# The prompt's last state built from the carried state: PE turns it back, ACT decays it, VectorE adds the second chunk's part

## The chip, the cores and the metric

One core of one Trainium2 chip runs the whole program. The metric is device time in microseconds (us), as the median of several runs. Below, PE is TensorE, DVE is VectorE, ACT is ScalarE, POOL is GpSimd, and SP is the queue that loads the weights.

## What is computed

One layer of a hybrid decoder: a Mamba-2 mixer beside a gated short convolution, then a gated ConvFFN and a gated per-layer embedding. There are 256 prompt tokens (one sequence, from a zero state) and 8 sequences of 8 sample tokens each, which makes 320 columns in all. The change concerns only the state that the prompt leaves behind. The prompt is worked off in two chunks of 128 tokens:

```python
decay_end = jnp.exp(Acum[:, :, -1:] - Acum)
chunk_states = jnp.einsum('bclgn,bclgr,bclgrp->bcgrpn', Bm, decay_end * dt, x)
chunk_decay = jnp.exp(Acum[:, :, -1])
def step(h, inp):
    s, d = inp
    return d[..., None, None] * h + s, h
hT, h_prev = lax.scan(step, h0.reshape(b, G, R, P, N), ...)
```

With a zero start and two chunks the last state is `hT = chunk_decay[1] * S0 + S1`, with S0 and S1 the two chunk states. S0 is also the state carried into the second chunk. There are 64 heads in 8 groups of 8. Per group a state has 512 rows (8 heads of 64) and 128 columns.

## The kernel before

All activations stand channel-major, so a projection is a matmul with a 128x128 block of weights held in the array and 320 token columns moving through. Weights come as f32 pieces of 128x1024. ACT rounds each piece to fp32r (`whi`, L670), DVE subtracts to get the rest (`wlo`, L1003), and PE does three matmuls for each block (L1567 to L1569). A `unit` is two such pieces, 48 matmuls, and gives 128 output channels.

The program is a hand-written list of steps (`ssm_steps`), which each engine walks through in its own block (`@block.scalar`, `@block.vector`, `@block.tensor` and so on). Each engine runs its part of a step in the order written there, and semaphores join them. The Mamba part is 8 rounds, one for each group of heads. Group 0 stands by itself and the other seven are a loop. A round ends with

`unit z0, ssd1, unit z1, ssd3, pair 0, unit z2, pair 1, unit z3, pair 2, pair 3`

- **dtab** (once, at the start): PE sums the decay exponents, ACT takes their exp, DVE multiplies. Kind 9 of `heads_tab` holds the weight of a first-chunk token in the last state: its PE sums go to bank 6 (two matmuls, L1880 and L1881), its exp is L852, its product with dt L1206.
- **ssd1**: PE turns x into rows of tokens. DVE scales them into `xdt` (for the output), `xwe` (for the end of their own chunk) and, for chunk 0 alone, `xwf` (for the end of the prompt, by kind 9).
- **ssd3**: PE turns the sample states of pair 0 (eight transposes, `turn_states`, L1774), makes the carried state S0 in bank 2 with one matmul of 512 columns (L1914), then the last state in bank 3, for each of four blocks of two heads `xwf` times chunk 0's B plus `xwe` times chunk 1's B (L1917, L1918: eight matmuls of 128 columns). ACT copies the turned states (L794), S0 into `h1t` (L906), the last state into `hfin` (L909), and issues its store (L911).
- **pair j** (two heads each): PE makes the outputs inside a chunk (L1931, bank 6), waits for `h1_kept` and `t_kept`, adds what the carried states give (L1942, L1946), and `carry_in` makes the samples' state updates in banks 7 and 2 (L1783). It then turns the next pair's sample states (L1774) and the pair's `yo` (L1955). ACT copies `yo` (L918) and the turned states, squares the pair's result, issues the load of the states two pairs on (L683) and the store of the new ones (L928). POOL decays the sample states (L1499), and DVE adds the update (L1256).

`HN_BANKS` is (7, 2): `carry_in` uses bank 7 for its first half and bank 2 for its second. `ea` holds, for each row of heads and each prompt column of chunk 1, exp of the running sum, so its column 127 is `chunk_decay[1]`.

Of the kernel before, what the change touches and what calls it, by code (L numbers as in the profile page):

```python
# [7 lines left out]
ACT = mybir.ActivationFunctionType  # L8

P = 128  # L10
# [3 lines left out]
NS = NB * LB  # L14
# [74 lines left out]
def ssm_steps(first):  # L89
    def x(*js):  # L90
        return [("unit", "x", j) for j in js]
    if first:
        head = (x(1) + [("dtend", 0)] + x(2) + [("dturn", 0)] + x(3) + [("dtab", 0)] + x(4)
                + [("bc", 0), ("decay", 0)] + x(5) + [("clamp", 0)])
        tail = [("unit", "z", 0), ("exps", 0), ("ssd1", 0), ("unit", "z", 1), ("mask", 0)]
    else:
        head = (x(0, 1) + [("norm", 0)] + x(2, 3) + [("bc", 0)] + x(4) + OUT8[:5] + [("decay", 0), ("clamp", 0)]
                + OUT8[5:6] + [("exps", 0)] + OUT8[6:] + [("mask", 0)] + x(5))
        tail = [("unit", "z", 0), ("ssd1", 0), ("unit", "z", 1)]
    return head + tail + [("ssd3", 0), ("pair", 0), ("unit", "z", 2), ("pair", 1), ("unit", "z", 3),  # L100
                          ("pair", 2), ("pair", 3)]

# [50 lines left out]
def hybrid_decoder(nc, ins, outs, scratch):  # L154
# [7 lines left out]
    with ctx:  # L162
        def sem(name):
            return ctx.enter_context(nc.semaphore(name))
# [38 lines left out]
        def s1(name, shape, dt=F32):  # L203
            return ssm.enter_context(nc.sbuf_tensor(name, shape, dt))

        N_KC = 10
        heads_tab = s1("heads_tab", [P, GROUPS, N_KC, HPG])
        hvec = s1("hvec", [HEADS, 3])  # L210
        dcol = s1("dcol", [P, HEADS // 2])
# [28 lines left out]
        cv = s1("cv", [P, 2, WX])  # L240
        xdt = s1("xdt", [P, 3, 4 * P])
        xwe = s1("xwe", [P, 3, 4 * P])
        xwf = s1("xwf", [P, 4 * P])
        bt = s1("bt", [P, 3, P])
        bblk = s1("bblk", [NS, NB // 2, P])
        cbm = s1("cbm", [P, 3, P])
# [111 lines left out]
        row_sums, rows_kept, rows_saved = sem("row_sums"), sem("rows_kept"), sem("rows_saved")  # L358
        acum_loaded, ea_loaded = sem("acum_loaded"), sem("ea_loaded")
        h1_done, h1_kept, hfin_stored = sem("h1_done"), sem("h1_kept"), sem("hfin_stored")  # L360
        h0_loaded = [sem(f"h0_loaded{i}") for i in range(2)]
        hn_stored = [sem(f"hn_stored{i}") for i in range(2)]
        t_done, t_kept = sem("t_done"), sem("t_kept")
# [30 lines left out]
        def at(i, n=1, size=1):  # L394
            return slice(i * size, (i + n) * size) if isinstance(i, int) else bass.ds(i * size, n * size)
# [255 lines left out]
        def _(act):  # L651
# [137 lines left out]
            def keep_states(g, j):  # L789

                wait(act, yo_done, 4 * g + j)
                for half in range(2):
                    act.wait_ge(t_done, 8 * g + 2 * j + half + 1)
                    activate(h0t[:, 4 * half:4 * half + 4, :].rearrange("p b n -> p (b n)"),  # L794
                             ps[:, 4 + half, :], copy).then_inc(t_kept, 1)

            def silu_x(g, i):

                act.wait_ge(conv_done, 6 * g + i + 1)

                wait(act, yg_ready, 4 * (g - 1) + (4 if i < 2 else i - 1))
                dst = bc[:, i, :] if i < 2 else xs[:, i - 2, :]
                activate(dst[:, 0:SEQ], prompt_of(cv[:, i % 2], K_X), ACT.Silu)
                if i == 1:
                    activate(c_own[:, :, :, 0:LB], samples_of(cv[:, i % 2], K_X).rearrange("p (h b) l -> p h b l", h=2),
                             ACT.Silu)
                activate(dst[:, SEQ:NT].rearrange("p (b l) -> p b l", l=LB), samples_of(cv[:, i % 2], K_X),
                         ACT.Silu).then_inc(xs_ready, 1)

            def tasks(seg, it, step, pos, outs_end):  # L810
# [34 lines left out]
                elif kind == "dtab":  # L845
# [2 lines left out]
                    activate(heads_tab[:, :, 3:5, :].rearrange("p g c h -> p c g h"),  # L848
                             ps[:, 5, 0:2 * HEADS].rearrange("p (c g h) -> p c g h", c=2, g=GROUPS), ACT.Exp)
                    activate(heads_tab[0:NS, :, 5, :],  # L850
                             ps[0:NS, 5, 2 * HEADS:3 * HEADS].rearrange("p (g h) -> p g h", g=GROUPS), ACT.Exp)
                    activate(heads_tab[:, :, 9, :],  # L852
                             ps[:, 6, 0:HEADS].rearrange("p (g h) -> p g h", g=GROUPS), ACT.Exp).then_inc(dt_decay, 1)
                    act.wait_ge(row_sums, 1)
                    activate(wm[0:HEADS, 2, 0:NT], ps[0:HEADS, 7, 0:NT], copy).then_inc(rows_kept, 1)
                    activate(wm[0:HEADS, 3, 0:P + NS + NB], ps[0:HEADS, 7, P:NT + NB], ACT.Exp).then_inc(rows_kept, 1)
# [41 lines left out]
                elif kind == "exps":  # L898
                    for quad in range(5):
                        act.wait_ge(q_pos, 5 * g + quad + 1)  # L900
                        part = wm[:, quad, :] if quad < 4 else wm[0:NS, quad, :]
                        activate(part, part, ACT.Exp, scale=-1.0).then_inc(q_exp, 1)
                elif kind == "ssd3":
                    keep_states(g, 0)
                    act.wait_ge(h1_done, 2 * g + 1)
                    activate(h1t[:], ps[:, 2, :], copy).then_inc(h1_kept, 1)  # L906
                    act.wait_ge(h1_done, 2 * g + 2)
                    wait(act, hfin_stored, 16 * g)
                    activate(hfin[:].rearrange("p q n -> p (q n)"), ps[:, 3, :], copy).then_inc(h1_kept, 1)  # L909
                    act.wait_ge(h1_kept, 2 * g + 2)  # L910
                    act.dma_start(outs["ssm_prompt"][0, 0].rearrange("h p n -> (h p) n")  # L911
                                  .rearrange("(q m) n -> m q n", m=P)[:, at(4 * g, 4)],
                                  hfin[:]).then_inc(hfin_stored, 16)
                elif kind == "pair":

                    wait(act, yoff_done, 4 * g + j)
# [1 line left out]
                    activate(yo[:], ps[:, YOFF_BANKS[j], P:2 * P], copy).then_inc(yo_kept, 1)  # L918
                    if j < 3:
                        keep_states(g, j + 1)  # L920
                    act.wait_ge(yg_ready, 4 * g + j + 1)
                    activate(zs[:, j, :], chunk[:, j, :], ACT.Square).then_inc(ysq_ready, 1)

# [70 lines left out]
        def _(dve):  # L994
# [167 lines left out]
            def tasks(seg, it, step, pos, outs_end):  # L1162
# [36 lines left out]
                elif kind == "dtab":  # L1199
# [5 lines left out]
                    tt(heads_tab[0:NS, :, 5, :], heads_tab[0:NS, :, 5, :], heads_tab[0:NS, :, 2, :], MUL)  # L1205
                    tt(heads_tab[:, :, 9, :], heads_tab[:, :, 9, :], heads_tab[:, :, 0, :], MUL  # L1206
                       ).then_inc(heads_ready, 1)
                elif kind == "unit" and step[1] == "x":
                    dve.wait_ge(xpad_filled, 6 * g + j + 1)
# [6 lines left out]
                elif kind == "ssd1":  # L1216
                    dve.wait_ge(hcol_ready, g + 1)
                    for c in range(3):
                        rows = P if c < 2 else NS
                        dve.wait_ge(xt_done, 3 * g + c + 1)  # L1220
                        xchunk(xdt[0:rows, c, :], c, hcol[0:rows, c, :], rows)
                        if c == 0:
                            xchunk(xwf[:], c, hcol[:, 9, :], rows)
                        xchunk(xwe[0:rows, c, :], c, hcol[0:rows, 3 + c, :], rows).then_inc(xw_ready, 1)
                elif kind == "bc":
                    dve.wait_ge(cb_done, g + 1)
# [9 lines left out]
                elif kind == "mask":  # L1236
                    dve.wait_ge(cbm_ready, g + 1)
                    for quad in range(5):
                        dve.wait_ge(q_exp, 5 * g + quad + 1)
                        c = CHUNK_OF[quad]  # L1240
                        rows, n = (P, 4) if quad < 4 else (NS, 8)
                        w3 = wm[0:rows, quad, :].rearrange("p (h n) -> p h n", h=n)
                        width = 512 // n
                        tt(w3, w3, cbm[0:rows, c, 0:width].unsqueeze(1).broadcast_to([rows, n, width]), MUL
                           ).then_inc(w_ready, 1)
                elif kind == "pair":
                    y = chunk[:, j, :]
                    dve.wait_ge(yd_done, 4 * g + j + 1)
# [313 lines left out]
        def _(pe):  # L1562
# [213 lines left out]

            def carry_in(g, j):

                for half in range(2):
                    if j:  # L1780
                        pe.wait_ge(hn_added, 8 * g + 2 * (j - 1) + half + 1)
                    rows = slice(half * NS // 2, (half + 1) * NS // 2)
                    mm(ps[:, HN_BANKS[half], :], xwe[rows, 2, j * P:(j + 1) * P],  # L1783
                       bblk[rows].rearrange("p b n -> p (b n)"), start=True, stop=True).then_inc(hn_done, 1)

            def tasks(seg, it, step, pos):
# [83 lines left out]
                elif kind == "dtab":  # L1870
# [5 lines left out]
                    for bank, inner, inner_s in ((4, tri[:], tri_s[:, 0:NS]), (5, after[:], after_s[:])):  # L1876
                        for c in range(2):
                            mm(ps[:, bank, c * HEADS:(c + 1) * HEADS], inner, dta(c, P), start=True, stop=True)
                        mm(ps[0:NS, bank, 2 * HEADS:3 * HEADS], inner_s, dta(2, NS), start=True, stop=True)
# [30 lines left out]
                elif kind == "ssd3":  # L1910
                    pe.wait_ge(xw_ready, 3 * g + 3)
                    pe.wait_ge(bt_kept, g + 1)
                    turn_states(g, 0)
                    mm(ps[:, 2, :], bt[:, 0, :], xwe[:, 0, :], start=True, stop=True).then_inc(h1_done, 1)  # L1914
                    for q in range(4):
                        cols = slice(q * P, (q + 1) * P)
                        mm(ps[:, 3, cols], xwf[:, cols], bt[:, 0, :], start=True, stop=False)  # L1917
                        last = mm(ps[:, 3, cols], xwe[:, 1, cols], bt[:, 1, :], start=False, stop=True)  # L1918
                    last.then_inc(h1_done, 1)
                elif kind == "pair":  # L1920
                    pe.wait_ge(w_ready, 5 * g + 5)
                    pe.wait_ge(cbm_ready, g + 1)
# [87 lines left out]
```

## Time and profile before

| | us |
|---|---|
| median of three runs | 2902.71 (2902.35 to 2904.03) |
| the profiled execution | 2901.83 |
| its span | 2900.1 |
| PE busy in the span | 2864.2 (99%) |
| DVE busy | 1718.3 (59%) |
| ACT busy | 1183.2 (41%) |
| POOL busy | 282.8 (10%) |

Busy time of PE is nearly the whole span. A matmul's row is longer than the step from one matmul's start to the next, since they overlap in the array. So what a matmul costs is read from starts, and a wait from a start that comes late.

### The profile page before, as it was taken

To read this page: it belongs to the slowest core of one execution; us is meant where nothing else is said; L and a number is where in the kernel's file an instruction comes from. 1 tells how busy PE (TensorE), PEld (TensorE's weight loads), DVE (VectorE), ACT (ScalarE), POOL (GpSimd) and SP (SyncE) were. 2 spreads that over 40 slices of the span, in tenths; PEclk is the share of its full clock that TensorE was granted. 3 is DMA by queue.
4 is the path that set the end of the run, shared out by engine and by line. 5 is a ranking of instruction groups with operands and counts; after the bars stand their busy time and mean duration, and the time that the engine had idled before them with its cause. 6 is when DMAs were issued, how large, how long until landed. Compare 5 with 4: busy or idle time off the path is not lost.

```text
span 2900.1 us, 52971 instructions
## 1 busy us (share of the span) xinstructions
PE 2864.2 (99%) x19924; PEld 2793.6 (96%) x19924; DVE 1718.3 (59%) x2165; ACT 1183.2 (41%) x1745; POOL 282.8 (10%) x447
## 2 busy tenths in 40 slices
PE   7999999999999999999999999999999999999998
PEld 6899999999999999999999999999999999999998
DVE  7676766767667655455455555655555555555564
ACT  4554544545445433333333334433333333333543
POOL 2211212112121200000000001000000000000100
PEclk9999999999999999999999999999999999999999
DMA  7666565665656655555555554555455555545463
GB/s 203 162 180 183 150 195 148 181 182 150 195 149 181 183 161 153 153 145 151 153 142 150 151 153 140 146 153 152 145 152 152 145 145 154 149 145 155 135 177 109
DMA packets 753280, 457.33 MB, mean 158 GB/s; under 512 B 14633, under 2 KB 747233, under 8 KB 752625
## 3 DMA queue, kind: packets, MB, share of 16 engines
q1 hardware_dynamic: 679433, 414.21, 50.5%
q10 hardware_dynamic: 73096, 39.39, 4.9%
q0 software_dynamic: 672, 2.66, 0.2%
q8 instruction: 52, 0.85, 0.1%
q14 instruction: 27, 0.22, 0.0%
HBM read 430.73 MB, written 25.47 MB: 157 GB/s over the span
## 4 chain that ended last, share of the span: by engine, by line
PE 96%; DVE 2%; ACT 1%; DMA 1%; issue 1%; POOL 0%; SPq 0%; ACTq 0%; DVEq 0%; POOLq 0%
PE ps L1567 29%; PE ps L1568 29%; PE ps L1569 29%; PE ps L1783 1%; PE ps L1774 1%; PE ps L1931 1%; PE ps L1946 1%; PE ps L1942 0%; PE ps L1800 0%; PE ps L1908 0%; PE ps L1679 0%; DVE wlo L1003 0%; PE ps L1689 0%; DMA raw<-in_w_in 0%; PE ps L1680 0%
## 5 line engine op out<-in xcount | busy, mean ns | idle before, releaser
L1567 PE MATMUL ps<-n_hi,whi 128*128 128x320 f32 x4144 | 1287.7, 311 | 2.5 <-issue 1.0
L1569 PE MATMUL ps<-n_hi,wlo 128*128 128x320 f32 x4144 | 1281.5, 309 | 0.0
L1568 PE MATMUL ps<-n_lo,whi 128*128 128x320 f32 x4144 | 1281.4, 309 | 0.0
L1003 DVE TENSOR_TENSOR wlo<-raw,whi 128x1024 fp32r<-128x1024 f32 x746 | 924.4, 1249 | 493.8 <-ACT whi L670 492.8
L670 ACT ACTIVATE whi<-raw 128x1024 fp32r<-128x1024 f32 x746 | 784.1, 1057 | 878.6 <-PE ps L1569 827.0
L1567 PEld LDWEIGHTS ps<-n_hi,whi 128*128 128x128 f32 x4144 | 778.8, 188 | 5.7 <-issue 3.1
L1568 PEld LDWEIGHTS ps<-n_lo,whi 128*128 128x128 f32 x4144 | 778.8, 188 | 0.6
L1569 PEld LDWEIGHTS ps<-n_hi,wlo 128*128 128x128 f32 x4144 | 778.6, 188 | 0.0
L1567 PE MATMUL ps<-c_hi,whi 128*128 128x320 f32 x1728 | 534.8, 310 | 0.5 <-DVE c_lo L1120 0.5
L1569 PE MATMUL ps<-c_hi,wlo 128*128 128x320 f32 x1728 | 534.0, 309 | 0.0
L1568 PE MATMUL ps<-c_lo,whi 128*128 128x320 f32 x1728 | 533.9, 309 | 0.0
L1567 PEld LDWEIGHTS ps<-c_hi,whi 128*128 128x128 f32 x1728 | 324.3, 188 | 1.0 <-DVE c_lo L1120 0.7
L1568 PEld LDWEIGHTS ps<-c_lo,whi 128*128 128x128 f32 x1728 | 324.4, 188 | 0.0
L1569 PEld LDWEIGHTS ps<-c_hi,wlo 128*128 128x128 f32 x1728 | 324.3, 188 | 0.0
L1286 DVE TENSOR_TENSOR xt<-xt,ps 128x640 f32<-128x640 f32 x120 | 98.6, 822 | 149.2 <-PE ps L1569 149.2
L787 ACT ACTIVATE c_hi<-chunk 128x320 fp32r<-128x320 f32 x76 | 35.9, 472 | 192.0 <-DVE chunk L1349 83.0
L1499 POOL TENSOR_TENSOR hn<-h,ea 128x512 f32<-128x512 f32 x64 | 71.7, 1145 | 239.7 <-DMA out_ssm_sample<-hn 239.7
L1442 POOL COPY ftail<-spad 128x18 f32 (+1 forms) x44 | 10.4, 235 | 860.4 <-ACT spad L960 860.4
L1286 DVE TENSOR_TENSOR acc_a<-acc_a,ps 128x640 f32<-128x640 f32 x64 | 52.5, 820 | 48.5 <-PE ps L1569 48.4
L1124 DVE TENSOR_SCALAR scv<-spad,scol 128x336 f32<-128x336 f32 x44 | 20.2, 460 | 86.2 <-ACT spad L960 86.2
L1127 DVE SCALAR_TENSOR_TENSOR cv<-xpad,gcol,cv 128x344 f32<-128x344 f32 x96 | 67.2, 700 | 3.4
L1256 DVE TENSOR_TENSOR hn<-hn,ps 128x512 f32<-128x512 f32 x64 | 41.1, 684 | 42.6 <-PE ps L1783 41.8
(292 smaller groups left out, 1772.2 us busy)
## 6 DMA issues: line engine op xcount, KB each, us to landing
raw<-in_w_in SPq DMA_DIRECT2D x322, 512.0 KB, 5.2
raw<-in_w_ffn_gate SPq DMA_DIRECT2D x88, 512.0 KB, 4.6
raw<-in_w_ffn_up SPq DMA_DIRECT2D x88, 512.0 KB, 5.0
raw<-in_w_ffn_down SPq DMA_DIRECT2D x88, 512.0 KB, 4.3
raw<-in_w_ssm_out SPq DMA_DIRECT2D x64, 512.0 KB, 4.3
h<-in_state_ssm ACTq DMA_DIRECT2D x32, 512.0 KB, 5.7
out_ssm_sample<-hn ACTq DMA_DIRECT2D x32, 512.0 KB, 4.6
raw<-in_w_sc_out SPq DMA_DIRECT2D x32, 512.0 KB, 4.1
```

The source lines that it names most:

```text
L670: activate(whi[slot][:], raw[slot][:], copy).then_inc(hi_split, 1)
L787: activate(c_hi[:, j, :], chunk[:, j, :], copy).then_inc(c_hi_ready, 1)
L1003: tt(wlo[slot][:], raw[slot][:], whi[slot][:].bitcast(F32), SUB).then_inc(lo_split, 1)
L1127: own(stt(dst, pad[:, k:k + n], weights[k], dst, MUL, ADD))
L1256: tt(hh, hh, ps[:, HN_BANKS[half], :], ADD).then_inc(hn_added, 1)
L1286: tt(dst, dst, ps[:, b0:b0 + 2, 0:NT], ADD).then_inc(out_added, 1)
L1499: g_.tensor_tensor(hn[j % 2][:, b, :], h0[j % 2][:, b, :], ea[:, j, P + NS + 4 * half:P + NS + 4 * half + 4].unsqueeze(2) .broadcast_to([P ...
L1567: mm(out, w_h, x_h, start=first, stop=False)
L1568: mm(out, w_h, x_l, start=False, stop=False)
L1569: return mm(out, w_l, x_h, start=False, stop=last)
L1774: last = turn(ps[:, 4 + half, b * P:(b + 1) * P], h0[j % 2][:, 4 * half + b, :], ident[:])
L1783: mm(ps[:, HN_BANKS[half], :], xwe[rows, 2, j * P:(j + 1) * P], bblk[rows].rearrange("p b n -> p (b n)"), start=True, stop=True).then_inc( ...
```

## The change

The kind 9 of the head table, `xwf` and the four matmuls with it are gone. In `ssd3` the carried state is now made first and the sample states are turned after it. A new step `last` stands between unit z2 and pair 1. In it PE turns the carried state `h1t` back (four transposes into bank 7) and makes the second chunk's part (four matmuls into bank 2). ACT copies bank 7 into `hfin` with the decay from `ea` as the scale, and DVE adds bank 2. The first use of banks 7 and 2 after that, `carry_in` of pair 1, waits for DVE's add. The store of `hfin` is issued by ACT within pair 1.

```diff
-    return head + tail + [("ssd3", 0), ("pair", 0), ("unit", "z", 2), ("pair", 1), ("unit", "z", 3),
+    return head + tail + [("ssd3", 0), ("pair", 0), ("unit", "z", 2), ("last", 0), ("pair", 1), ("unit", "z", 3),
...
-        N_KC = 10
+        N_KC = 9
...
-        xwf = s1("xwf", [P, 4 * P])
...
+            def store_last(g):
+
+                act.wait_ge(last_kept, g + 1)
+                act.dma_start(outs["ssm_prompt"][0, 0].rearrange("h p n -> (h p) n")
+                              .rearrange("(q m) n -> m q n", m=P)[:, at(4 * g, 4)],
+                              hfin[:]).then_inc(hfin_stored, 16)
...
-                    activate(heads_tab[:, :, 9, :],
-                             ps[:, 6, 0:HEADS].rearrange("p (g h) -> p g h", g=GROUPS), ACT.Exp).then_inc(dt_decay, 1)
...
                 elif kind == "ssd3":
-                    keep_states(g, 0)
-                    act.wait_ge(h1_done, 2 * g + 1)
+                    act.wait_ge(h1_done, g + 1)
                     activate(h1t[:], ps[:, 2, :], copy).then_inc(h1_kept, 1)
-                    act.wait_ge(h1_done, 2 * g + 2)
+                    keep_states(g, 0)
+                elif kind == "last":
+                    act.wait_ge(last_done, 2 * g + 1)
+                    act.wait_ge(ea_loaded, 32 * (g + 1))
                     wait(act, hfin_stored, 16 * g)
-                    activate(hfin[:].rearrange("p q n -> p (q n)"), ps[:, 3, :], copy).then_inc(h1_kept, 1)
-                    act.wait_ge(h1_kept, 2 * g + 2)
...
+                    for q in range(4):
+                        last = activate(hfin[:, q, :], ps[:, HN_BANKS[0], q * P:(q + 1) * P], copy,
+                                        scale=ea[:, q, P - 1:P])
+                    last.then_inc(last_decayed, 1)
...
                     if j < 3:
                         keep_states(g, j + 1)
+                    if j == 1:
+                        store_last(g)
...
-                        if c == 0:
-                            xchunk(xwf[:], c, hcol[:, 9, :], rows)
...
+                elif kind == "last":
+                    dve.wait_ge(last_done, 2 * g + 2)
+                    dve.wait_ge(last_decayed, g + 1)
+                    of_all = hfin[:].rearrange("p q n -> p (q n)")
+                    tt(of_all, of_all, ps[:, HN_BANKS[1], :], ADD).then_inc(last_kept, 1)
...
             def carry_in(g, j):
 
+                if j == 1:
+                    pe.wait_ge(last_kept, g + 1)
...
-                    mm(ps[:, 6, 0:HEADS], after[:], dta(0, P), start=True, stop=False)
-                    mm(ps[:, 6, 0:HEADS], ones[:], dta(1, P), start=False, stop=True).then_inc(dt_sums, 1)
...
+                    mm(ps[:, 2, :], bt[:, 0, :], xwe[:, 0, :], start=True, stop=True).then_inc(h1_done, 1)
                     turn_states(g, 0)
-                    mm(ps[:, 2, :], bt[:, 0, :], xwe[:, 0, :], start=True, stop=True).then_inc(h1_done, 1)
+                elif kind == "last":
+                    pe.wait_ge(hn_added, 8 * g + 2)
                     for q in range(4):
-                        cols = slice(q * P, (q + 1) * P)
-                        mm(ps[:, 3, cols], xwf[:, cols], bt[:, 0, :], start=True, stop=False)
-                        last = mm(ps[:, 3, cols], xwe[:, 1, cols], bt[:, 1, :], start=False, stop=True)
-                    last.then_inc(h1_done, 1)
+                        last = turn(ps[:, HN_BANKS[0], q * P:(q + 1) * P], h1t[:, q * P:(q + 1) * P], ident[:])
+                    last.then_inc(last_done, 1)
+                    for q in range(4):
+                        last = mm(ps[:, HN_BANKS[1], q * P:(q + 1) * P], xwe[:, 1, q * P:(q + 1) * P], bt[:, 1, :],
+                                  start=True, stop=True)
+                    last.then_inc(last_done, 1)
...
-                    pe.wait_ge(h1_kept, 2 * g + 2)
+                    pe.wait_ge(h1_kept, g + 1)
```

PE from the end of unit z1 to the carried state's first use in pair 0, before:

```order
L1774 MATMUL ps<-ident,h_0 128x128 [waits h0_loaded0,bt_kept,xw_ready]
L1774 MATMUL ps<-ident,h_0 128x128 x7
L1914 MATMUL ps<-xwe,bt 128x512
L1917 MATMUL ps<-bt,xwf 128x128
L1918 MATMUL ps<-bt,xwe 128x128
L1917 MATMUL ps<-bt,xwf 128x128
L1918 MATMUL ps<-bt,xwe 128x128
...
L1931 MATMUL ps<-wm,xdt 64x128 [waits cbm_ready,w_ready]
L1931 MATMUL ps<-wm,xdt 64x128 x3
L1931 MATMUL ps<-wm,xdt 64x64 x2
L1942 MATMUL ps<-bc,h1t 128x128 [waits t_kept,h1_kept]
```

and with the change:

```order
L1925 MATMUL ps<-xwe,bt 128x512 [waits bt_kept,xw_ready]
L1785 MATMUL ps<-ident,h_0 128x128 [waits h0_loaded0]
L1785 MATMUL ps<-ident,h_0 128x128 x7
L1947 MATMUL ps<-wm,xdt 64x128 [waits cbm_ready,w_ready]
L1947 MATMUL ps<-wm,xdt 64x128 x3
L1947 MATMUL ps<-wm,xdt 64x64 x2
L1958 MATMUL ps<-bc,h1t 128x128 [waits t_kept,h1_kept]
```

Eight matmuls are gone between the sample turns and pair 0, and the one of 512 columns stands ahead of the turns. The wait before L1942 (now L1958) is for the same two semaphores.

PE after unit z2, with the change (before, L1931 followed z2 directly, and L1783 waited for `hn_added` and `bblk_ready` alone):

```order
L1930 MATMUL ps<-ident,h1t 128x128 [waits hn_added]
L1930 MATMUL ps<-ident,h1t 128x128 x3
L1933 MATMUL ps<-bt,xwe 128x128 x4
L1947 MATMUL ps<-wm,xdt 64x128 [waits hn_added,cbm_ready,w_ready]
L1947 MATMUL ps<-wm,xdt 64x128 x3
L1947 MATMUL ps<-wm,xdt 64x64 x2
L1958 MATMUL ps<-bc,h1t 128x128 [waits yg_ready,t_kept,h1_kept]
L1962 MATMUL ps<-h0t,c_own 32x128 x8
L1796 MATMUL ps<-bblk,xwe 128x512 [waits hn_added,last_kept,bblk_ready]
L1796 MATMUL ps<-bblk,xwe 128x512 [waits hn_added]
```

Eight PE instructions come in ahead of pair 1, and `carry_in` has the wait for `last_kept`.

ACT from the copy of z2's result to the square of pair 1, with the change:

```order
L893 ACTIVATE zs<-ps 128x320 [waits multiplied]
L918 ACTIVATE hfin<-ps,ea 128x128 [waits ea_loaded,last_done]
L918 ACTIVATE hfin<-ps,ea 128x128 x3
L925 ACTIVATE yo<-ps 128x128 [waits yo_done,yoff_done]
L794 ACTIVATE h0t<-ps 128x512 [waits t_done,yo_done]
L794 ACTIVATE h0t<-ps 128x512 [waits t_done]
L800 DMA out_ssm_prompt<-hfin 128x4x128 [waits last_kept]
L931 ACTIVATE zs<-chunk 128x320 [waits yg_ready]
L683 DMA h_1<-in_state_ssm 128x8x128 [waits hd_done]
L937 DMA out_ssm_sample<-hn 128x8x128 [waits hn_added]
```

The four decaying copies and the store are new here; both stood, as L909 and L911, in `ssd3` of before.

## Rows read from the trace of the kernel before

**Rows 1.** The page's part on the chain that ended last, by engine.

```profile
PE 96%; DVE 2%; ACT 1%; DMA 1%; issue 1%; POOL 0%; SPq 0%; ACTq 0%; DVEq 0%; POOLq 0%
```

**Rows 2.** Windows: busy us of each engine, granted clock, DMA share, GB/s.

```profile
66.00:71.50 5.50, 5.50 (x24) 5.33 (x25) 5.39 (x11) 0.00 (x0) 0.00 (x0) 0.50 0.63 166
...
590.00:630.00 40.00, 39.91 (x334) 33.24 (x333) 21.03 (x36) 14.45 (x25) 5.82 (x6) 1.00 0.61 171
```

**Rows 3.** Timeline of PE in group 4, unit z1's end to pair 0: start, length, instruction.

```profile
595.68 1.04 PE L1774 MATMUL ps<-ident,h 128*128 128x128 f32 x8
596.55 1.02 PE L1914 MATMUL ps<-xwe,bt 128*128 128x512 f32 x2
597.41 0.38 PE L1917 MATMUL ps<-bt,xwf 128*128 128x128 f32 x2
597.63 0.39 PE L1918 MATMUL ps<-bt,xwe 128*128 128x128 f32 x2
...
599.29 0.92 PE L1931 MATMUL ps<-wm,xdt 128*64 128x128 f32 x12
600.20 0.48 PE L1942 MATMUL ps<-bc,h1t 128*128 128x128 f32 x2
```

**Rows 4.** Timeline of PE in group 4, pair 1.

```profile
610.42 0.92 PE L1931 MATMUL ps<-wm,xdt 128*64 128x128 f32 x12
611.27 0.49 PE L1942 MATMUL ps<-bc,h1t 128*128 128x128 f32 x2
...
612.26 1.13 PE L1783 MATMUL ps<-bblk,xwe 32*128 32x512 f32 x4
613.32 1.09 PE L1774 MATMUL ps<-ident,h 128*128 128x128 f32 x8
```

**Rows 5.** Timeline of ACT in group 4, from ssd3 to pair 1.

```profile
597.61 0.60 ACT L906 ACTIVATE h1t<-ps 128x512 f32<-128x512 f32 x1 [0.21 <-PE ps L1914]
599.48 0.60 ACT L909 ACTIVATE hfin<-ps 128x512 f32<-128x512 f32 x1 [1.27 <-PE ps L1918]
...
610.53 0.44 ACT L887 ACTIVATE zs<-ps 128x320 f32<-128x320 f32 x1 [2.20 <-PE ps L1569]
612.40 0.28 ACT L918 ACTIVATE yo<-ps 128x128 f32<-128x128 f32 x1 [1.44 <-PE ps L1946]
614.01 1.09 ACT L794 ACTIVATE h0t<-ps 128x512 f32<-128x512 f32 x2 [1.34 <-PE ps L1774]
...
616.27 0.38 ACTq L683 DMA_DIRECT2D h<-in_state_ssm  x1
```

**Rows 6.** Timelines of DVE and of POOL in group 4, pair 1.

```profile
613.42 1.28 DVE L1256 TENSOR_TENSOR hn<-hn,ps 128x512 f32<-128x512 f32 x2 [1.49 <-PE ps L1783]
...
611.68 2.04 POOL L1499 TENSOR_TENSOR hn<-h,ea 128x512 f32<-128x512 f32 x2 [25.30 <-DMA out_ssm_sample<-hn]
```

**Rows 7.** Timelines of DVE and PE in group 0, unit z1 to pair 0.

```profile
109.43 2.34 DVE L1003 TENSOR_TENSOR wlo<-raw,whi 128x1024 fp32r<-128x1024 f32 x2
111.70 3.08 DVE L1244 TENSOR_TENSOR wm<-wm,cbm 128x512 f32<-128x512 f32 x5
...
114.87 0.92 PE L1931 MATMUL ps<-wm,xdt 128*64 128x128 f32 x12
```

**Rows 8.** Timeline of ACT in step dtab.

```profile
78.90 0.21 ACT L852 ACTIVATE heads_tab<-ps 128x64 f32<-128x64 f32 x1
79.29 0.43 ACT L855 ACTIVATE wm<-ps 64x320 f32<-64x320 f32 x1 [0.18 <-PE ps L1884]
```

**Rows 9.** Waits of PE: who waited for whom, us in total, times, longest.

```profile
PE ps L1867 <- DVE wm L1191: 4.4, 1, 4.4
...
PE ps L1908 <- ACT xs L807: 1.1, 1, 1.1
```

**Rows 10.** DMA issues at 616 to 626 us: KB each, us to landing.

```profile
h<-in_state_ssm ACTq DMA_DIRECT2D x1, 512.0 KB, 4.6
```

More of the change, by code:

```diff
@@ L360, in hybrid_decoder @@
         h1_done, h1_kept, hfin_stored = sem("h1_done"), sem("h1_kept"), sem("hfin_stored")
+        last_done, last_decayed, last_kept = sem("last_done"), sem("last_decayed"), sem("last_kept")
         h0_loaded = [sem(f"h0_loaded{i}") for i in range(2)]
@@ L850, in tasks @@
                     activate(heads_tab[0:NS, :, 5, :],
-                             ps[0:NS, 5, 2 * HEADS:3 * HEADS].rearrange("p (g h) -> p g h", g=GROUPS), ACT.Exp)
-                    activate(heads_tab[:, :, 9, :],
-                             ps[:, 6, 0:HEADS].rearrange("p (g h) -> p g h", g=GROUPS), ACT.Exp).then_inc(dt_decay, 1)
+                             ps[0:NS, 5, 2 * HEADS:3 * HEADS].rearrange("p (g h) -> p g h", g=GROUPS), ACT.Exp
+                             ).then_inc(dt_decay, 1)
                     act.wait_ge(row_sums, 1)
@@ L903, in tasks @@
                 elif kind == "ssd3":
+                    act.wait_ge(h1_done, g + 1)
+                    activate(h1t[:], ps[:, 2, :], copy).then_inc(h1_kept, 1)
                     keep_states(g, 0)
-                    act.wait_ge(h1_done, 2 * g + 1)
-                    activate(h1t[:], ps[:, 2, :], copy).then_inc(h1_kept, 1)
-                    act.wait_ge(h1_done, 2 * g + 2)
+                elif kind == "last":
+                    act.wait_ge(last_done, 2 * g + 1)
+                    act.wait_ge(ea_loaded, 32 * (g + 1))
                     wait(act, hfin_stored, 16 * g)
-                    activate(hfin[:].rearrange("p q n -> p (q n)"), ps[:, 3, :], copy).then_inc(h1_kept, 1)
-                    act.wait_ge(h1_kept, 2 * g + 2)
-                    act.dma_start(outs["ssm_prompt"][0, 0].rearrange("h p n -> (h p) n")
-                                  .rearrange("(q m) n -> m q n", m=P)[:, at(4 * g, 4)],
-                                  hfin[:]).then_inc(hfin_stored, 16)
+                    for q in range(4):
+                        last = activate(hfin[:, q, :], ps[:, HN_BANKS[0], q * P:(q + 1) * P], copy,
+                                        scale=ea[:, q, P - 1:P])
+                    last.then_inc(last_decayed, 1)
                 elif kind == "pair":
@@ L1204, in tasks @@
                         tt(heads_tab[:, :, 3 + c, :], heads_tab[:, :, 3 + c, :], heads_tab[:, :, c, :], MUL)
-                    tt(heads_tab[0:NS, :, 5, :], heads_tab[0:NS, :, 5, :], heads_tab[0:NS, :, 2, :], MUL)
-                    tt(heads_tab[:, :, 9, :], heads_tab[:, :, 9, :], heads_tab[:, :, 0, :], MUL
+                    tt(heads_tab[0:NS, :, 5, :], heads_tab[0:NS, :, 5, :], heads_tab[0:NS, :, 2, :], MUL
                        ).then_inc(heads_ready, 1)
@@ L1878, in tasks @@
                             mm(ps[:, bank, c * HEADS:(c + 1) * HEADS], inner, dta(c, P), start=True, stop=True)
-                        mm(ps[0:NS, bank, 2 * HEADS:3 * HEADS], inner_s, dta(2, NS), start=True, stop=True)
-                    mm(ps[:, 6, 0:HEADS], after[:], dta(0, P), start=True, stop=False)
-                    mm(ps[:, 6, 0:HEADS], ones[:], dta(1, P), start=False, stop=True).then_inc(dt_sums, 1)
+                        last = mm(ps[0:NS, bank, 2 * HEADS:3 * HEADS], inner_s, dta(2, NS), start=True, stop=True)
+                    last.then_inc(dt_sums, 1)
                     for c in range(2):
```

## The prediction

> **What bounds the kernel now.** I read first the chain that ended last: PE holds 96% of it [rows 1], so a change pays or costs what it does to PE's sequence of starts, and work on ACT, DVE or POOL counts only where PE comes to wait for it. The windows say at what clock that sequence runs: in the stretch around `ssd3` and the first pairs of group 4 the granted clock is 1.00, full speed, and PE is busy 39.91 of 40 us [rows 2]. Then I read PE's own timeline at the two places that the change touches, from start to start [rows 3, 4], and beside it ACT, DVE and POOL, to see when each is free [rows 5, 6]. Group 0 stands outside the loop and has other work beside it, so it is read by itself [rows 7]. The steps of a pair come again 11.07 us later (L1942 at 600.20 and at 611.27 [rows 3, 4]), and the eight groups look alike but for group 0.
>
> **Part 1, `ssd3`, groups 1 to 7: PE gains 1.76 us each.** Before, from the first turn (595.68) to the first use of the carried state (L1942, 600.20) is 4.52 us [rows 3]. In it are eight turns (0.87, so 0.11 each), the matmul of 512 columns (0.86), eight matmuls of 128 columns (0.22 each, 597.41 to 597.63), 0.10 before pair 0 starts at 599.29, and 0.91 up to L1942. In pair 1 that last piece takes 0.85 (610.42 to 611.27 [rows 4]); the 0.06 more in pair 0 is a wait for ACT's `hfin` copy, which ends at 600.08, 0.12 before L1942 starts [rows 3, 5].
> With the change PE's own work here is 0.86 + 0.87 + 0.10 + 0.85 = 2.68. The cover of 1.8 us that the eight matmuls gave ACT is gone, so I follow ACT, counting from the start of the 512 matmul. It can copy `h1t` at 1.06 (597.61 less 596.55 [rows 3, 5]). A copy behind another takes 0.49 more (two take 1.09 and one 0.60 [rows 5]), so the first `h0t` copy can start at 1.55. That is also when its four turns are through: ACT starts 0.69 after the first turn does (614.01 less 613.32 [rows 4, 5]), and 0.86 + 0.69 = 1.55. The two copies end at 2.64, and with the 0.12 from a copy's end to PE's start L1942 comes at 2.76. ACT is thus late by 0.08, and the gain is 4.52 - 2.76 = 1.76.
>
> **Part 2, step `last`: PE pays 1.33 us in each of 8 groups.** Four turns at 0.11 are 0.44, and four matmuls at 0.22 are 0.89 [rows 3]. The step's wait for `hn_added` asks for adds of pair 0, a whole unit earlier, and costs nothing. The gap before pair 1 stays as it is.
>
> **The added wait, on `last_kept` before `carry_in` of pair 1, costs nothing by my sum, with 0.6 us to spare.** Count from the end of z2, 610.33 (pair 1 starts 0.09 behind it [rows 4]). PE reaches `carry_in` at 1.33 + 0.09 + 1.84 = 3.26, where 1.84 is 610.42 to 612.26 [rows 4]. Meanwhile:
> - ACT's copy of z2's result ends at 0.64 (610.53 + 0.44 [rows 5]); the turns are through for ACT at 0.69. The four decaying copies have no row. A bound from below is one copy of the same 512 columns, 0.60; from above four of those, 2.4. A copy of 128x128, the same shape without the decay, takes 0.28 [rows 5]. I take 1.1, four times that, since it is the nearest row. They end at 1.8.
> - DVE's add reads one operand from PSUM and one from SBUF, 128x512, as L1256 does: 1.28 for two, 0.68 for one [rows 6]. It waits for `last`'s matmuls too (1.33 plus the array's tail, under 0.3: a 128-column matmul's row of 0.38 holds two steps of 0.11 [rows 3]). So it runs from about 1.9 to 2.55, and PE may go on at about 2.65.
> With the upper bound of 2.4 for ACT, PE would go on at 3.95 and wait 0.7. DVE's next work, the pair's `chunk`, is queued behind this add: it is ready at 1.42 + 0.85 and the array's tail, about 2.5, so it slips by 0.1 at most, and PE asks for it a unit later.
>
> **Work that moves beside PE.** DVE's `xwf` product (0.6) goes and the add comes, POOL copies eight columns less. ACT does 1.1 instead of 0.6, in time in which it idles 1.44 before `yo` [rows 5]. The store of `hfin` (256 KB) moves from pair 0 into pair 1 on ACT's queue, behind the turned states' copies and ahead of the load of pair 3's states. ACT is idle there until the square, so its issue delays no copy. The load is issued at 616.27 and lands 4.6 us later, at 620.9 [rows 5, 10]. Its turns are one period behind those at 613.32, at about 624.4, so 3.5 us are to spare, and the load's own 4.6 for twice the bytes says that a store of half the size in front costs about 2.3. Nothing, then, on PE. SP's queue is not touched.
>
> **Part 3, group 0: PE pays 0.73 us in sum.** Here pair 0 also needs DVE's masks: the last one ends at 114.78, and PE starts pair 0 at 114.87 [rows 7]. In the other groups the masks come long before. Today PE's eight matmuls fill just that time. Without them PE waits, and the masks come earlier by no more than the 0.6 us of `xwf` on DVE, since the parts at 109.43 follow the products at once [rows 7]. So `ssd3` gives 0.60 here instead of 1.76, and `last` costs its 1.33. Bound: if ACT's halves of the weights hold DVE up, the 0.60 falls to 0.
>
> **Part 4, `dtab`: 0.37 us gained.** PE does two small matmuls less, and ACT one exp. PE then meets its wait of 1.1 us for ACT's `xs` [rows 9], so its own time is not gained. ACT's is: L855 starts at 79.29, after L852 (78.90) and a wait of 0.18 for PE [rows 8]. With both gone it can start near 78.92. Behind it stand the copies that are saved for all groups and the loads that ACT later waits for, up to that `xs`. Bounds: 0 and 0.37; I take the 0.37, as one chain leads through.
>
> **Sum.** 7 x (1.33 - 1.76) + 0.73 - 0.37 = -3.01 + 0.36 = **-2.65 us**. The profiled execution took 2901.83, which would become 2899.2. The median of the runs shown is 0.88 above it: 2902.7 - 2.65 = **2900.1**. That is 0.09% less. A measurement of this kernel tells from no change about 0.2%, 5.8 us, so I call it no change that can be told.
>
> **The rivals.**
> - *Every microsecond of PE counts* (the masks, ACT's copies and `dtab` hold nothing up): 8 x 0.45 and about 0.5 in `dtab`, 2898.6. Against it stands the mask's end so close to PE's start [rows 7]. Chance 0.10.
> - *The wait takes the gain's place.* With ACT's copies near their upper bound, PE waits 0.7 in each group: +5.6, so 2905.7. Between that and my sum lie smaller waits. Chance 0.10.
> - *Slower: POOL holds DVE's add.* POOL decays pair 2's states from 611.68 to 613.72 [rows 6], 1.35 to 3.39 after z2's end, just when the add wants to run at 1.9. If the add had to wait for POOL's end, it would end at 4.07 and PE go on at 4.19 instead of 3.26: 0.93 in each group, 7.4 in all, giving 2907.5. With ACT's copies slow as well it passes 0.2%. It decides once the add starts later than 2.5. For it speaks the overlap in time; against it that the two adds L1256 began at 613.42, with POOL still at work, and took 1.28 as they do elsewhere [rows 6]. Chance 0.08.
> - *Slower: the clock falls.* In the start-up the granted clock was 0.50, the lower level of 1.2 GHz, from 66 to 71.5 us, and ahead of it PE had idled 4.4 us [rows 2, 9]. Such a stretch loses half of 5.5, 2.75 us; in every group that would be 22 us, 2922. But PE idles nowhere near that long in a group, and around eight turns in a pair the clock stays 1.00 [rows 2]. Chance 0.02.
> - *The freed time on DVE and ACT opens something I don't see*, or the turns cost less than in `ssd3`: below 2896.9. I see no mechanism; 0.05.
> My forecast keeps 0.65.
>
> On the clock the Trainium skill (TensorE: Matmul & The Clock Gate, Part 4: PE-mode transpose) speaks against the change: a transpose doesn't count as PE work for the clock as a matmul does, and the change puts transposes in the place of matmuls. By that rule the clock could fall, toward 2922; by the row, with 1.00 around eight turns in a pair, the sum stays at 2900.1. On POOL and DVE the skill (SBUF — State Buffer, Who interferes with whom) states that a DVE instruction with at most one SBUF input does not contend with GpSimd. By that the add is not held and the sum stands; the row of the two L1256 agrees, as far as 0.3 us of overlap can show it.
>
> **Range and chances.** From below, every microsecond counts and the runs scatter by 1 us: 2897.5. From above, the wait near its bound: 2905.7. Faster by over 0.2%: 0.07, the last rival and a tail of the first. Slower by over 0.2% (above 2908.5): 0.07, the clock, and POOL with slow copies. Within 0.2%: 0.86.
>
> **What would show it.** In the profile after, L1958 stands 2.7 to 2.8 us after the first instruction behind z1, with ACT's `h0t` copy named as what it waited for. The four `hfin` copies take about 1.1 in sum and start 0.7 after z2. `carry_in` in pair 1 starts 3.2 to 3.3 after z2's end, with no wait on DVE. In group 0 pair 0 starts right behind the last mask. The period from one group to the next shrinks by 0.4. The prediction is wrong if that period grows, if `carry_in` waits for `last_kept`, or if the clock falls in a pair.

## The result, and the profile after

The changed kernel is slower: 2931.6 us as the median (2922.06 to 2934.28), against 2902.61 (2901.97 to 2904.03) for the kernel before on the same chip. The ratio is 1.0093 (95% interval 1.0083 to 1.0104), so +0.9%, where I had forecast 2900.1 and a range up to 2905.7. The profiled execution took 2926.92 us, with a span of 2925.2.

First the rows that answer to [rows 3] and [rows 4]: PE's timeline in group 4, behind unit z1 and behind unit z2.

```profile
604.25 1.02 PE L1925 MATMUL ps<-xwe,bt 128*128 128x512 f32 x2
605.10 1.04 PE L1785 MATMUL ps<-ident,h 128*128 128x128 f32 x8
606.07 0.92 PE L1947 MATMUL ps<-wm,xdt 128*64 128x128 f32 x12
...
606.93 0.49 PE L1958 MATMUL ps<-bc,h1t 128*128 128x128 f32 x2
...
617.06 0.60 PE L1930 MATMUL ps<-ident,h1t 128*128 128x128 f32 x4
617.50 1.06 PE L1933 MATMUL ps<-bt,xwe 128*128 128x128 f32 x8
618.48 0.92 PE L1947 MATMUL ps<-wm,xdt 128*64 128x128 f32 x12
...
620.33 1.13 PE L1796 MATMUL ps<-bblk,xwe 32*128 32x512 f32 x4
```

Everything the change touches goes as forecast here: L1958 comes 2.68 us after the 512-column matmul (forecast 2.7 to 2.8), `last` holds PE from 617.06 to 618.48, and `carry_in` starts 3.27 after z2's end (forecast 3.2 to 3.3), with no wait in its row. Yet the next group's 512-column matmul comes at 729.24, 124.99 later. Before, the same step is 717.36 less 596.55, 120.81. The two rows, after and then before:

```profile
729.24 1.02 PE L1925 MATMUL ps<-xwe,bt 128*128 128x512 f32 x2
```

```profile
717.36 1.02 PE L1914 MATMUL ps<-xwe,bt 128*128 128x512 f32 x2
```

So 4 us and more are lost in a round, and not at any place that the diff touches.

The waits of PE name the place. Columns: who waited, for whom, us in total, times, longest. First the kernel before, then after.

```profile
PE ps L1567 <- issue: 1.0, 1, 1.0
```

```profile
PE ps L1578 <- issue: 17.6, 7, 4.4
```

"issue" means that PE waited for nothing that the profile shows. One of the seven in PE's timeline, at the loop's back edge: `pair 3` of group 4's round has ended, and the first matmul of the next round is late.

```profile
761.47 0.33 PE L1971 MATMUL ps<-ident,yo 128*128 128x128 f32 x1
766.21 0.63 PE L1578 MATMUL ps<-n_hi,whi 128*128 128x320 f32 x1 [4.41 <-issue]
766.63 0.47 PE L1579 MATMUL ps<-n_lo,whi 128*128 128x320 f32 x1
766.90 0.47 PE L1580 MATMUL ps<-n_hi,wlo 128*128 128x320 f32 x1
767.17 0.47 PE L1578 MATMUL ps<-n_hi,whi 128*128 128x320 f32 x1
767.43 0.47 PE L1579 MATMUL ps<-n_lo,whi 128*128 128x320 f32 x1
```

Six of them stand at the back edge (1.8 to 4.4 us each, 16.6 in sum), where a round ends and the branch leads back to the next. The seventh, 1.0, comes at 1044.87, 30 us after the loop's last pair. Behind each of the six the matmuls come at 0.27 us instead of 0.15 for a while, and the windows show why. Columns: window, length, busy us of PE, its weight loads, DVE, ACT, POOL, the granted clock, DMA share, GB/s.

```profile
761.85:766.15 4.30, 0.00 (x0) 0.00 (x0) 2.29 (x6) 1.30 (x2) 1.25 (x5) 0.78 0.52 143
766.20:771.00 4.80, 4.79 (x17) 4.60 (x18) 1.23 (x1) 0.17 (x1) 0.11 (x1) 0.50 0.58 157
771.00:776.00 5.00, 5.00 (x36) 5.00 (x35) 1.23 (x1) 1.06 (x1) 0.00 (x0) 0.99 0.99 318
```

While PE is idle for 4.4 us the granted clock falls to 0.50, the lower level of 1.2 GHz, and stays there for another 4.8 us, which loses 2.4. Idle and clock make 6.8 us for this round. The period from group 5's 512-column matmul to group 6's, which holds this stretch, is 126.89, against 120.80 to 120.85 before: 6.1 more, or 6.5 with the 0.4 that the change was to gain.

What PE waited for shows in the DMA queues. The page's part 3 lists one queue of instructions with packets of 16 KB. Whole run, before and then after:

```profile
q8 instruction: 52, 0.85, 0.1%
```

```profile
q8 instruction: 106, 1.74, 0.3%
```

By windows of 120 us from 240 to 960, inside the loop, before has 1, 0, 0, 0, 0, 0 packets of instructions and after 8, 9, 9, 9, 8, 9: 51 of the 54 that it has more. The same answer for 720 to 840 us, before (no q8 row at all) and after:

```profile
## 3 DMA queue, kind: packets, MB, share of 16 engines
q1 hardware_dynamic: 25527, 16.08, 47.0%
q10 hardware_dynamic: 8848, 4.46, 13.8%
```

```profile
## 3 DMA queue, kind: packets, MB, share of 16 engines
q1 hardware_dynamic: 23840, 15.22, 44.5%
q10 hardware_dynamic: 8848, 4.46, 13.7%
q8 instruction: 8, 0.13, 0.5%
```

Before, the last packet of the loop comes before 266 us, in its first round, so PE went through the other six rounds on instructions it had. After, packets come in every round. One falls into the stretch ahead of 766.21. The answer for 761.8 to 766.2 us has the row

```profile
q8 instruction: 1, 0.02, 1.3%
```

For the stretch of 2.2 us that ends at 639.00, the window from 635.8 to 636.1 us has one packet too:

```profile
q8 instruction: 1, 0.02, 27.7%
```

At 766.21 the packet comes 1.6 us after PE has gone idle, and the stretch takes 4.4. At 639.00 it comes 0.7 us or more before PE goes idle, and the stretch takes 2.2. At all six back edges the first matmul starts 2.8 to 3.2 us behind such a packet, so the stretch is short where the packet comes early. From this I take it that PE fetches its instructions again in every round, and that the branch back waits for the first packet.

### The profile page after: what moved, and what is told of

It reads as the page before. It is cut to its first block, busy times and chain, and to the rows that moved or that the text cites. A ratio compares the mean times of both kernels' runs of the same rounds, so it can differ in the third digit from the quotient of the medians.

```text
span 2925.2 us, 52937 instructions
## 1 busy us (share of the span) xinstructions
PE 2872.2 (98%) x19888; PEld 2801.3 (96%) x19888; DVE 1718.8 (59%) x2164; ACT 1186.7 (41%) x1768; POOL 281.9 (10%) x447
## 4 chain that ended last, share of the span: by engine, by line
PE 95%; DVE 2%; issue 1%; ACT 1%; DMA 1%; POOL 0%; SPq 0%; ACTq 0%; DVEq 0%; POOLq 0%
PE ps L1578 29%; PE ps L1579 29%; PE ps L1580 29%; PE ps L1796 1%; PE ps L1785 1%; PE ps L1947 1%; PE ps L1962 1%; PE ps L1958 0%; DVE wlo L1012 0%; PE ps L1813 0%; DMA raw<-in_w_in 0%; PE ps L1690 0%; PE ps L1920 0%; PE ps L1700 0%; PE ps L1691 0%
## 5 line engine op out<-in xcount | busy, mean ns | idle before, releaser
L1578 PE MATMUL ps<-n_hi,whi 128*128 128x320 f32 x4144 | 1293.4, 312 | 17.4 <-issue 16.6
L1453 POOL COPY xtail<-xpad 128x27 f32 (+1 forms) x48 | 25.6, 534 | 418.3 <-ACT xpad L883 418.3
```

What stands on the lines that cost most here:

```text
L1453: g_.tensor_copy(tail[:, :, :, at(t)].rearrange("p i k a -> p i (k a)"), last_rows(pad, taps)).then_inc(kept, 1)
L1578: mm(out, w_h, x_h, start=first, stop=False)
```

## The experiments

```diff
-                return nc.Fori(seg.start, seg.stop, engines=[eng.engine], hint_back_edge=True)
+                return nc.Fori(seg.start, seg.stop, engines=[eng.engine], hint_back_edge=True,
+                               head_slot={eng.engine: 0})
```

> The changed kernel, its computation untouched; only PE's loop of the groups 1 to 7 is told at which slot of a fetch block its first instruction is laid (slot 0). Theory F (fetch): the 29 us come from instruction fetches at the loop's end. The trace of the changed kernel has 7 idle stretches of PE put down to issue, 17.6 us in all, each before the first matmul of a round, the granted clock at 0.50 behind most of them, and 8 or 9 instruction packets of 16 KB in every round, where the kernel before had none from its third group on. The code ahead of the loop is 16 instructions shorter than before and the loop 8 shorter, so only its place differs to the bad. Then slot 0 gives 2899 to 2901 us, no instruction packets in the rounds, and the period of a round at 120.4. Theory W (wait): the cost is made inside the round by the added wait or by the clock falling over the transposes; then this stays at 2922 to 2934. The Trainium skill (Runtime: NRT & Kernel Launch, Instruction fetch mechanics) gives PE an instruction memory of 2048 instructions in blocks of 256; the loop's 1838 instructions fit in 8 blocks at slot 0.

Measured 2897.9 (2896.46 to 2900.07), ratio 0.9983 (0.9974 to 0.9992), a little under the 2899 to 2901 expected. No stretch named "issue" over 0.3 us, and the queue's row is that of before:

```profile
q8 instruction: 52, 0.85, 0.1%
```

The period is 120.28 (six times, within 0.02). With nothing else changed, 33.7 us are back: the theory holds, rival A falls.

**e2: the kernel before, head at slot 224.**

> The kernel before, nothing of the change in it, with PE's loop laid at slot 224 of a block, so that its 1846 instructions reach over 9 blocks instead of 8. Theory F: 2925 to 2937 us, with 8 or 9 instruction packets in every round and 2 to 4 us of idle PE at the head of each. Theory W, which ties the cost to the step last: 2901 to 2904, as before.

Measured 2933.25 (2921.84 to 2938.44), ratio 1.0091 (1.0073 to 1.0109). The old code shows the same loss when its 1846 instructions start at 224:

```profile
PE ps L1568 <- issue: 24.2, 7, 4.4
```

**e3 and e4: the changed kernel, head at slots 210 and 211.** 210 + 1838 is 2048, so 210 is the last slot at which the body ends within eight blocks.

> The changed kernel with its loop at slot 210: 210 + 1838 = 2048 instructions, the last slot at which the loop still stands in 8 blocks of 256. Theory F: 2899 to 2901, as at slot 0, with no packets in the rounds. Theory W: no difference from 2922 to 2934 here either.

> The changed kernel with its loop one slot further, at 211, so that its last instruction stands in a ninth block. Theory F in its strict form (eight blocks are kept, nine make every block be fetched again in every round): 2922 to 2934, 22 us or more above slot 210 for one slot. A looser rival (what matters is the distance of the branch from its target, or how the hint is laid): no jump between 210 and 211.

Measured 2905.75 (2905.14 to 2908.53) at 210 and 2936.87 (2935.47 to 2937.59) at 211: one slot is worth 31 us, in two programs that differ by nothing else. Rival B falls with that. (For 211 the expectation had 2922 to 2934, at least 22 above slot 210.) The rows on waits and the instruction queue, of e3 and then of e4:

```profile
PE ps L1579 <- issue: 5.9, 4, 4.0
```

```profile
q8 instruction: 53, 0.87, 0.1%
```

```profile
PE ps L1579 <- issue: 28.0, 9, 4.4
```

```profile
q8 instruction: 107, 1.75, 0.3%
```

In e3 no packet falls between 240 and 960 us, and the period is 120.27. Its 7.9 us over slot 0 were not expected (2899 to 2901 was). The two profiled executions show where time goes: a stretch of 4.0 right behind the loop's last pair, the clock at 0.50 for 4.7 us behind it (2.3 lost), a stretch of 0.7 at 1023.11, and a first period that is 0.75 longer, 7.8 in sum. Why leaving the loop costs more from slot 210 stays open.

```profile
991.33 0.61 PE L1579 MATMUL ps<-n_hi,whi 128*128 128x320 f32 x1 [4.02 <-issue]
991.74 0.47 PE L1580 MATMUL ps<-n_lo,whi 128*128 128x320 f32 x1
```

That the limit is eight blocks is what the Trainium skill's size for PE gives (Runtime: NRT & Kernel Launch, Instruction fetch mechanics: 128 KiB, 2048 instructions, in blocks of 16 KiB); these two runs agree to the instruction. The same section calls the memory a FIFO with two lines (a number it works out from the 32 KiB of the other engines), and says that a taken branch out of a window of two pages forces a fetch. If that held for PE, every round of every version would fetch. The kernel before, e1 and e3 show no fetch in the loop after its first round, so the measurement decides: with the hint on, all eight blocks stay.

**e5 and e7: only the number of instructions ahead of the loop.** e5 gives the changed kernel 16 instructions back that do nothing of use; e7 takes 16 from the kernel before (group 0's four matmuls with `xwf`, so that group's last state lacks its first chunk's part). No slot is told in either.

```diff
+                    for _ in range(8):
+                        turn(ps[:, 7, P:2 * P], ident[:], ident[:])
```

```diff
-                        mm(ps[:, 3, cols], xwf[:, cols], bt[:, 0, :], start=True, stop=False)
-                        last = mm(ps[:, 3, cols], xwe[:, 1, cols], bt[:, 1, :], start=False, stop=True)
+                        if seg.start:
+                            mm(ps[:, 3, cols], xwf[:, cols], bt[:, 0, :], start=True, stop=False)
+                        last = mm(ps[:, 3, cols], xwe[:, 1, cols], bt[:, 1, :], start=not seg.start, stop=True)
```

> The changed kernel with eight more transposes of the identity at PE's very start (into a part of bank 7 that nothing reads then), which are 16 instructions and about 1 us, so that the loop begins as many instructions into PE's program as in the kernel before, and no slot is given. Theory F: the loop's place is what it was before, so 2898 to 2902 us and no packets in the rounds from the third group on. If a told slot had some merit of its own that made the run at slot 0 fast, this stays at 2922 to 2937.

> The kernel before without the four xwf matmuls of group 0 alone, so the last state of group 0 lacks its first chunk's part. They are 16 instructions (a matmul of f32 data is two pairs of load and multiply), ahead of the loop, and leave 0.9 us of work out. Nothing else of the change is in it: no step last, no added wait, no transposes. Theory F: the loop now begins where it does in the changed kernel, so 2922 to 2937, with 8 or 9 packets in every round. Theory W: 2901 to 2903.

| ahead of the loop | body before (1846) | body after (1838) |
|---|---|---|
| 1716 | 2902.61 (before) | 2898.77 (e5; 2897.25 to 2902.4) |
| 1700 | 2929.8 (e7; 2927.57 to 2933.99) | 2931.6 (after) |

The row decides and the column hardly matters. Leaving work out made the kernel before 27 us slower, and adding useless work made the changed one 33 us faster. That is the cause, shown from both sides. Where the loader puts the two unforced heads I did not read from any row. The four runs bound it, if 16 instructions move a head by 16 slots: both bodies fit where before's head is, and neither fits 16 slots further back, so before's head is at a slot from 0 to 15 and after's at one from 240 to 255. (1716 by itself, in blocks of 256, would give 180; the counted program can't begin at the start of a block.) Before's packets, which fall as in e1, agree.

**e6: the kernel before at slot 0**, to see the change's own worth with both loops at one place.

> The kernel before with its loop at slot 0, the fair base for the changed kernel at slot 0 (2897.9). If the loop of the kernel before stands well by itself: 2901 to 2904, and the change is worth 4 to 5 us. If slot 0 itself gave part of those 4.2 us (the kernel before has an idle stretch of 1.0 at its first round's end that the changed one at slot 0 has not), this is at 2899 to 2901 and the change is worth 2 to 3, as my sum had it.

Measured 2901.39 (2900.46 to 2903.47). Against e1's 2897.9 the change itself is worth -3.5 us, between the two values that I had expected (4 to 5, or 2 to 3). The two ran on different chips; set against the kernel before on its own chip (2902.12 and 2902.76), e1 gains 4.2 and e6 1.4, which makes -2.9 for the change. The period goes from 120.82 to 120.28, -0.54.

**e8, e9, e10: the hint for the branch back left out.** e8 is e1, e9 is e6 and e10 is e2 with `hint_back_edge=False` on PE's loop. (e9's expectation speaks of every engine that loops; the edit touches PE's alone.)

> The changed kernel at slot 0 with the branch hint of its loop taken out. If all eight blocks stay in the instruction memory from round to round, the hint has nothing to fetch: 2897 to 2899, equal to slot 0 with it. If the hint is what hides the fetch at the loop's end, 2 to 4 us of idle PE come back in each of seven rounds, and with the clock behind them 2920 or more.

> The kernel before, its loop's head at slot 0 as in the run that gave 2901.39, and the hint for the branch back left out on every engine that loops. The changed kernel at slot 0 went from 2897.9 to a median of 2909.4 between 2896.6 and 2922.8 without the hint, with instruction fetches of 4.1 to 4.4 us in three rounds of seven. If that comes from the missing hint, the kernel before must show it too: 2904 to 2916 with runs up to 20 us apart, fetches in some rounds, none in others. If it was a chance of that one program, 2899 to 2903, and no packets of instructions in the middle of the loop.

> The kernel before with the head at slot 224, so that the loop spans nine blocks, and no hint. With the hint this took 2933.25, with eight or nine packets of instructions in each round. If the hint starts part of that fetch early, leaving it out makes it longer: 2936 to 2960. If at nine blocks all is fetched in any case and PE's stretches are the fetch itself, the hint is worth nothing here: 2930 to 2938.

| | with the hint | without |
|---|---|---|
| after, slot 0 (e1, e8) | 2897.9 | 2909.38 (2896.62 to 2922.78) |
| before, slot 0 (e6, e9) | 2901.39 | 2935.41 (2930.56 to 2936.62) |
| before, slot 224 (e2, e10) | 2933.25 | 2940.8 (2939.17 to 2942.3) |

My expectation for e8 (2897 to 2899) missed, and e9 was underrated (2904 to 2916 expected). The instruction queue of e8 and of e9, whole run:

```profile
q8 instruction: 79, 1.29, 0.2%
```

```profile
q8 instruction: 97, 1.59, 0.2%
```

Without the hint a loop that fits is fetched again too: at three of the six back edges in e8's profiled execution, at five in e9's. The rounds of e8 without a stretch take 120.19 to 120.24, even a little less than the 120.28 with the hint. Only the runs with both, a body within eight blocks and the hint, show no fetch at any back edge. Fitting alone does not ensure it, though one run of e8 took 2896.62, as little as e1's fastest. What decides, without the hint, whether a round fetches stays open. At nine blocks the medians with and without the hint lie 7.6 us apart, as the first branch of e10's expectation had it. But the four runs of e2 scatter by 17 and e4, with the hint, took 2936.87, so the size of that is not settled. What the traces show is that stretches of 1.8 to 2.4 us, with the packet ahead of PE's idle time, occur with the hint alone: four in after, three in e7, one in e2, though none in e4. The 14 stretches at the back edges of e8, e9 and e10 take 4.1 to 4.4 each.

## Why the prediction was wrong

The terms can be read in e1, the changed kernel without the fetch. Its lines stand one further down than after's. ACT, DVE and POOL in group 4, around `ssd3` and `last`:

```profile
597.56 1.08 ACT L795 ACTIVATE h0t<-ps 128x512 f32<-128x512 f32 x2
...
609.62 1.14 ACT L919 ACTIVATE hfin<-ps,ea 128x128 f32<-128x128 f32 x4 [0.16 <-PE ps L1931]
...
614.41 0.40 ACTq L801 DMA_DIRECT2D out_ssm_prompt<-hfin  x1
```

```profile
610.87 0.69 DVE L1257 TENSOR_TENSOR hfin<-hfin,ps 128x512 f32<-128x512 f32 x1 [2.59 <-ACT hfin L919]
611.47 0.54 DVE L1263 SCALAR_TENSOR_TENSOR chunk<-xs,gd,ps 128x320 f32<-128x320 f32 x1
```

```profile
610.48 2.04 POOL L1511 TENSOR_TENSOR hn<-h,ea 128x512 f32<-128x512 f32 x2 [23.77 <-DMA out_ssm_sample<-hn]
```

- **Part 1, right.** The carried state is first used 2.69 us behind z1 (596.01 to 598.70 in e1), 2.76 forecast: a gain of 1.83 for 1.76. The 0.08 of lateness does not show: ACT's copies end at 598.64 and no wait is named.
- **Part 2, right.** `last` costs 1.33: 608.83 to 610.25 in e1, less the 0.09 ahead of pair 1. `carry_in` starts at 612.09, 3.26 after z2's end, as forecast.
- **The added wait, right.** The four decaying copies start 0.79 after z2's end (0.69 forecast) and take 1.14 in sum (1.1). The add ends at 2.73 (2.55 forecast), 0.5 before `carry_in`. `chunk` follows at once.
- **Rival "POOL holds DVE's add", refuted.** The add runs inside POOL's 2.04 us and takes 0.69, like one of L1256's before. On that the Trainium skill's rule (SBUF — State Buffer, Who interferes with whom) and this run agree.
- **Part 3, right.** In group 0 PE now waits for the last mask, which ends at 115.99. From z1's end to pair 0 it is 2.99 (113.06 to 116.05), before 3.61 (111.26 to 114.87): 0.62 gained for 0.60.

```profile
112.90 3.09 DVE L1251 TENSOR_TENSOR wm<-wm,cbm 128x512 f32<-128x512 f32 x5
...
116.05 0.92 PE L1948 MATMUL ps<-wm,xdt 128*64 128x128 f32 x12 [1.09 <-DVE wm L1251]
```

- **Part 4, right.** From PE's wait for `wm` in `dtab` to the unit that waits for ACT's `xs` it is 36.56 us (65.59 to 102.15, in after), before 36.92 (65.93 to 102.85): -0.36 for -0.37.
- **The sum, right for what it counted:** -2.65 forecast, -3.5 between e6 and e1, or -2.9 with each set against its own chip's kernel before. Seven rounds at -0.54 against my -0.43 make 0.8 of the difference.
- **Rivals "every microsecond of PE counts" and "the wait takes the gain's place", refuted.** The masks do hold PE up in group 0, for 1.09, and `carry_in` has no wait in e1. That the change's worth comes near the first rival's -4.1 is chance.
- **Rival "the clock falls": it fell, for another reason and for less.** The rival had 22 us, all of it from the clock, and its 2922 is near the measured time by luck. Over the six periods behind a back edge the changed kernel takes 28.8 us more than e1's 120.28 each; 16.6 are idle time, which no rival had, and 12.2 the low clock. It falls while PE is idle at the back edge and stays at 1.00 around the turns, as the window of after over pairs 0 and 1 of group 4 shows:

```profile
603.00:625.00 22.00, 22.00 (x184) 18.53 (x183) 9.43 (x18) 9.28 (x19) 2.23 (x3) 1.00 0.56 156
```

  The Trainium skill's rule on transposes (TensorE: Matmul & The Clock Gate, Part 4: PE-mode transpose) is not what acted here: e1 has the same transposes, and no such fall.

**The step that failed** is the one before the sum: I took the sequence of PE's starts as everything that PE does. That the change makes PE's code ahead of the loop shorter by 16 instructions, and the body by 8, was no term of the sum and no rival; it was free in my account. It cost 33.7 us (e1 against after), over twelve times the whole sum. The profile of before held a hint of it, which I didn't read: 51 of its 52 packets of instructions lie outside 240 to 960 us, so that the loop was running on instructions already held. With the size that the experiments then bore out, 1846 in 2048, its head may lie at slots 0 to 202 alone. From that a rival would have followed, though no row of before has its price. That the head did cross the edge could not be read from the timeline in any case.

## What to carry to other kernels

If a loop's body nearly fills what an engine holds of its instructions, count them on every edit, ahead of the loop as well as in it, and fix the place of its head; here slot 0 and the hint made the changed kernel the fastest version run (2897.9 us, 0.17% under the kernel before), and the change a small gain. When a kernel gets slower by the same few us in every round and the edited places run as planned, look at the back edge for idle time put down to "issue", and at the instruction queue's packets by window. A slowdown that comes with an edit can be undone by 16 instructions of padding, which tells nothing against the edit.

## What the runs showed of the hardware that I had not expected

- One slot decides 31 us in seven rounds (e3, e4). With nine blocks, eight or nine packets of 16 KB come in every round, not just the one that doesn't fit.
- A fetch at the back edge costs PE 1.8 to 4.4 us of idle time, and the low clock behind it 1.5 to 2.6 us more (after, each round's period less 120.28 and less its stretch).
- A loop that fits is refetched without the hint (e8, e9), and not in every round.
- Leaving the loop can cost a stretch too: 4.0 us in e3, none in e1. A packet of instructions falls about 2.4 us ahead of the end of that stretch.
- A 128x128 copy by ACT takes 0.28 us without a scale [rows 5]; with one scale for each partition 369 ns as the mean of 32, and four back to back take 1.14 in sum.
